# An output filled with the offset row before the normalised rows are added to it: the tail of a mixture-of-experts layer

## What is computed

```python
proj = x @ w_in                                  # 1024 x 2560
y    = concat(rg_lru(conv4(rg_x)) * gelu(rg_gate), sc_b * conv3(sc_c * sc_v))
h    = layer_norm(alpha * x + y @ w_out, ln1_g, ln1_b)
# router: the best of 4 groups, then the best 2 of its 8 experts; combine = their weights
hid  = silu(h @ exp_w_gate[e]) * (h @ exp_w_up[e]) * combine    # 32 experts, 1024 x 256 each
ffn  = sum_e hid_e @ exp_w_down[e]                              # 256 x 1024 each
out  = layer_norm(alpha * h + ffn, ln2_g, ln2_b)  # (z - mean) * rstd * ln2_g + ln2_b
```

## Time and profile before

| | |
|---|---|
| runs, median (lowest to highest) | 427.05 us (426.9 to 427.5) |
| the profiled execution, its own time | 426.65 us |
| its span in the trace | 424.9 us |
| granted TensorE clock over the span | 0.987 of 2.4 GHz |
| TensorE, VectorE, ScalarE, GpSimd busy | 96%, 48%, 22%, 21% of the span |
| moved by DMA | 137.03 MB, mean 323 GB/s |

### The profile page before, as it was taken

How to read it: one execution, slowest core, us unless ns; L and a number is a source line. 1 busy time by engine, 2 the same in 40 slices (tenths; PEclk the granted TensorE clock), 3 DMA queues, 4 the chain that set the end, 5 groups by cost and what they waited for, 6 DMA issues and landing times.

```text
span 424.9 us, 6858 instructions
## 1 busy us (share of the span) xinstructions
PE 406.7 (96%) x2734; PEld 277.6 (65%) x2734; DVE 205.6 (48%) x401; ACT 95.1 (22%) x148; POOL 89.4 (21%) x130
## 2 busy tenths in 40 slices
PE   6999999999999999998999999999999999798993
PEld 5888877888888888965556555555655655454541
DVE  1579622399957458775623322332332332232167
ACT  3533466984114001410000000000000000001031
POOL 3220000000000001053333233223323323311024
PEclk8999999999999999999999999999999999899998
DMA  8776421320269999989999999999999999999965
GB/s 275 243 216 199 150 89 61 99 79 21 99 202 398 420 422 414 422 343 410 417 416 416 412 415 413 412 416 415 413 417 419 416 415 419 416 420 413 395 267 197
DMA packets 37426, 137.03 MB, mean 323 GB/s; under 512 B 5155, under 2 KB 17475, under 8 KB 25366
## 3 DMA queue, kind: packets, MB, share of 16 engines
q1 hardware_dynamic: 31232, 124.79, 74.0%
q0 software_dynamic: 6144, 11.84, 7.8%
q10 hardware_dynamic: 22, 0.02, 0.0%
HBM read 132.31 MB, written 12.58 MB: 341 GB/s over the span
## 4 chain that ended last, share of the span: by engine, by line
PE 84%; DMA 10%; DVE 3%; SPq 1%; issue 1%; ACT 0%; POOL 0%; DVEq 0%; POOLq 0%
PE bank L1176 23%; PE bank L978 12%; PE bank L980 12%; PE bank L979 12%; PE bank L1205 11%; DMA wgu_spare<-in_exp_w_up 7%; PE bank L1164 3%; PE bank L1196 3%; PE bank L1221 2%; DMA xg<-h_rows,x_rows 2%; PE bank L1316 1%; PE bank L1075 1%; DMA raw<-in_w_in 1%; PE bank L1087 1%; PE bank L1038 1%
## 5 line engine op out<-in xcount | busy, mean ns | idle before, releaser
L1176 PE MATMUL bank<-wgu,xTg 128*64 128x256 f32 x736 | 86.0, 387 | 2.9 <-DMA wgu<-in_exp_w_up 2.9
L1176 PEld LDWEIGHTS bank<-wgu,xTg 128*64 128x64 f32 x736 | 51.6, 139 | 30.3 <-DMA wgu<-in_exp_w_up 3.2
L978 PE MATMUL bank<-xT_hi,w_hi 128*128 128x512 f32 x160 | 63.2, 395 | 1.7 <-DVE xT_lo L1380 1.7
L1699 DVE TENSOR_TENSOR hid<-hid,bank 64x256 f32<-64x256 f32 x32 | 13.5, 423 | 104.3 <-ACT hid L920 104.2
L980 PE MATMUL bank<-xT_hi,w_lo 128*128 128x512 f32 x160 | 62.8, 392 | 0.0
L979 PE MATMUL bank<-xT_lo,w_hi 128*128 128x512 f32 x160 | 62.8, 392 | 0.0
L743 POOL DMA_INDIRECT y_pairs<-xg,y_rows x32 | 31.9, 998 | 120.3 <-DVE xg L1709 114.5
L920 ACT ACTIVATE hid<-bank 64x256 f32<-64x256 f32 x32 | 12.0, 375 | 194.5 <-PE bank L1176 185.5
L1205 PE MATMUL bank<-wdn,hidT 128*64 128x512 f32 x192 | 45.4, 593 | 0.2 <-issue 0.2
L1357 DVE TENSOR_TENSOR w_lo<-raw,w_hi 128x2048 fp32r<-128x2048 f32 x12 | 27.5, 2289 | 26.9 <-ACT w_hi L834 26.7
L978 PEld LDWEIGHTS bank<-xT_hi,w_hi 128*128 128x128 f32 x160 | 30.2, 189 | 9.5 <-issue 3.4
(11 more groups left out here) (274 smaller groups left out, 497.3 us busy)
## 6 DMA issues: line engine op xcount, KB each, us to landing
wgu<-in_exp_w_gate SPq DMA_DIRECT2D x24, 1024.0 KB, 18.7
wgu<-in_exp_w_up SPq DMA_DIRECT2D x24, 1024.0 KB, 21.1
wdn<-in_exp_w_down SPq DMA_DIRECT2D x24, 1024.0 KB, 21.0
raw<-in_w_in SPq DMA_DIRECT2D x9, 1024.0 KB, 6.2
raw<-in_w_out SPq DMA_DIRECT2D x4, 1024.0 KB, 5.0
wdn_extra<-in_exp_w_down SPq DMA_DIRECT2D x4, 1024.0 KB, 20.7
wgu_spare<-in_exp_w_gate SPq DMA_DIRECT2D x4, 1024.0 KB, 21.7
wgu_spare<-in_exp_w_up SPq DMA_DIRECT2D x4, 1024.0 KB, 23.7
```

The source lines that it names most:

```text
L978: pe.matmul(dst, a_hi, b_hi, start=start, stop=False)
L1176: mm = pe.matmul(psum[2 + b][BLOCK * which:BLOCK * which + BLOCK, 0:F], xTg[b][:, j, h * BLOCK:(h + 1) * BLOCK], wgu[s][:, which, k, :], s ...
```

## The change

- SP issues eight stores inside the loop of chunk loads, behind chunks 4 to 11: each writes 64 rows of the output in HBM with the row `ln2_b`, 256 KB from HBM to HBM. The load of `ln2b` is gone.
- The normalised rows no longer get the offset on an engine. GpSimd issues the stores, with accumulation in the DMA (`accum_op=ALU.add`), onto the filled output. It waits once for the fills, and it ends with the wait for all stores.
- Columns 512 to 1023 of tiles 0 to 2, and columns 0 to 511 of tile 3, get their last scaling on ScalarE; the other half of tile 3 on VectorE. GpSimd has one operation for a tile where it had two.
- Item 31's gate and up pieces are loaded ahead of item 30's down weights. TensorE sums item 31's gate and up right behind item 30's, with item 30's transposition in the middle (`between`), and item 30's down behind that.
- The result of items 30 and 31 is kept as two fp32r parts, high by ScalarE and low by VectorE (`split_last`), and `last_hotT` is fp32r. Each of the two products of an `add_last` call becomes two, with one pass each. The four calls for item 30 and tiles 0 and 1, which stood around item 31's transposition, now come behind item 31's down.

```diff
             for c in range(1, N_CHUNKS):
...
+                if 4 <= c < 4 + 2 * TT:
+                    sp_.dma_start(out_rows[(c - 4) * BLOCK:(c - 3) * BLOCK, :], row(ln2_b).to_broadcast([BLOCK, D])).then_inc(out_filled, 16)
...
             refill_gu(N_EXP - 2)
-            refill_dn(N_EXP - 2)
             sp_.wait_ge(gu_summed, LAST - RING + 1)
...
+            refill_dn(N_EXP - 2)
             refill_dn(LAST)
...
-                    sp_.dma_start(ln2b[:, :], row(ln2_b).to_broadcast([P, D])).then_inc(ln2b_in, 16)
...
-            for t in range(TT - 1):
-                sp_.wait_ge(out_ready_pool, t + 1)
-                sp_.wait_ge(out_ready, t + 1)
-                sp_.dma_start(out_rows[t * P:(t + 1) * P, :], pair_y[2 * t + 1][:, :]).then_inc(out_stored, 16)
-            for h in range(2):
-                sp_.wait_ge(out_ready, TT + h)
-                cols = slice(h * H, (h + 1) * H)
-                sp_.dma_start(out_rows[(TT - 1) * P:, cols], pair_y[2 * TT - 1][:, cols]).then_inc(out_stored, 16)
-            sp_.wait_ge(out_stored, 16 * (TT + 1))
...
+            pool.wait_ge(out_filled, 16 * 2 * TT)
             for t in range(TT - 1):
...
-                pool.tensor_tensor(z, z, ln2b[:, 0:H], ALU.add).then_inc(out_ready_pool, 1)
+                pool.wait_ge(out_ready, t + 1)
+                pool.dma_start(out_rows[t * P:(t + 1) * P, :], z[:, :], accum_op=ALU.add).then_inc(out_stored, 16)
+            for h in range(2):
+                cols = slice(h * H, (h + 1) * H)
+                pool.wait_ge((out_ready, out_ready_last)[h], (TT, 1)[h])
+                pool.dma_start(out_rows[(TT - 1) * P:, cols], pair_y[2 * TT - 1][:, cols], accum_op=ALU.add).then_inc(out_stored, 16)
+            pool.wait_ge(out_stored, 16 * (TT + 1))
...
             rounds(act, act_item)
+            act.wait_ge(slot_weight_ready, 1)
+            copy_last(0)
             copy_last(1)
...
+                h = 0 if t == TT - 1 else 1
+                act.wait_ge(rstd2_ready, t + 1)
+                act.wait_ge(scaled2_ready, t + 1)
+                act.activation(pair_y[2 * t + 1][:, h * H:(h + 1) * H], z_of(t, h), ACT.Copy, scale=rstd[:, t:t + 1]).then_inc(out_ready, 1)
...
+                    if between is not None and k == KT // 2:
+                        between()
...
-                    pe.matmul(part_of(z_of(t, h), a), last_hotT[n][rows, t, :], last_y[n][rows, h * F:(h + 1) * F],
-                              start=first and turn == 0, stop=done is not None).then_inc(last_half_added if done is None else done, 1)
+                    pe.matmul(part_of(z_of(t, h), a), last_hotT[n][rows, t, :], last_y_hi[n][rows, h * F:(h + 1) * F],
+                              start=first and turn == 0, stop=False)
+                    pe.matmul(part_of(z_of(t, h), a), last_hotT[n][rows, t, :], last_y_lo[n][rows, h * F:(h + 1) * F],
+                              start=False, stop=done is not None).then_inc(last_half_added if done is None else done, 1)
...
                     gate_up(q, slot_of(q), q % 2, 2, loads_of(q, r))
-                    turn_hid(q, q % 2, 2)
                     return
                 if static(r) and q == LAST:
+                    gate_up(q, slot_of(q), q % 2, 2, loads_of(q, r), last_gu_in, lambda: turn_hid(q - 1, (q - 1) % 2, 2))
                     main_down(q - 1, r)
-                    gate_up(q, slot_of(q), q % 2, 2, loads_of(q, r), last_gu_in)
-                    pe.wait_ge(last_hotT_ready, 2)
-                    pe.wait_ge(last_y_copied, 1)
-                    add_last(0, 0, 0, True)
-                    add_last(0, 1, 0, True)
                     turn_hid(q, q % 2, 2)
-                    add_last(0, 0, 1, True)
-                    add_last(0, 1, 1, True)
                     return
...
             main_down(N_EXP - 1, 0)
+            pe.wait_ge(last_hotT_ready, 2)
+            pe.wait_ge(last_y_lo_ready, 1)
+            for turn in range(2):
+                for t in range(2):
+                    add_last(0, t, turn, True)
...
+            def split_last(n):
+                i = DIRECT[n]
+                v.wait_ge(last_y_hi_ready, n + 1)
+                v.scalar_tensor_tensor(out=last_y_lo[n][:, :], in0=psum[6 + i % 2][:, :], scalar=slot_weight[:, i:i + 1], in1=last_y_hi[n][:, :],
+                                       op0=ALU.mult, op1=ALU.subtract).then_inc(last_y_lo_ready, 1)
...
-                for h in halves:
-                    cols = slice(h * H, (h + 1) * H)
-                    v.scalar_tensor_tensor(out=pair_y[2 * t + 1][:, cols], in0=z_of(t, h), scalar=rstd[:, t:t + 1], in1=ln2b[:, cols],
-                                           op0=ALU.mult, op1=ALU.add).then_inc(out_ready, 1)
+                else:
+                    v.wait_ge(dve, chain[0])
+                    v.tensor_scalar(pair_y[2 * t + 1][:, H:D], z_of(t, 1), rstd[:, t:t + 1], None, ALU.mult).then_inc(out_ready_last, 1)
```

More of the change, by code:

```diff
@@ L255, in hybrid_moe_layer @@
         th = [tanhs[:, j, :] for j in range(3)] + [tanh3[:, :]]
-        last_hot = [at(f"last_hot{n}", [P, TT, 2, BLOCK], F32, ring + SLOT + 6144 * n) for n in range(2)]
-        last_hotT = [at(f"last_hotT{n}", [P, TT, P], F32, ring + SLOT + 6144 * n + 2048) for n in range(2)]
-        last_y = [at(f"last_y{n}", [P, H], F32, ring + SLOT + 6144 * n + 4096) for n in range(2)]
+        last_hot = [at(f"last_hot{n}", [P, TT, 2, BLOCK], F32, ring + SLOT + 8192 * n) for n in range(2)]
+        last_hotT = [at(f"last_hotT{n}", [P, TT, P], F32R, ring + SLOT + 8192 * n + 2048) for n in range(2)]
+        last_y_hi = [at(f"last_y_hi{n}", [P, H], F32R, ring + SLOT + 8192 * n + 4096) for n in range(2)]
+        last_y_lo = [at(f"last_y_lo{n}", [P, H], F32R, ring + SLOT + 8192 * n + 6144) for n in range(2)]
         ln2g = at("ln2g", [P, D], F32, ring + SLOT + 16384)
-        ln2b = at("ln2b", [P, D], F32, ring + SLOT + 20480)
         pair_y = [at(f"pair_y{u}", [P, D], F32, ring + 2 * SLOT + 4096 * u) for u in range(2 * TT)]
@@ L309, in hybrid_moe_layer @@
         ln2g_in = sem("ln2g_in")
-        ln2b_in = sem("ln2b_in")
+        out_filled = sem("out_filled")
         router_in = sem("router_in")
@@ L402, in hybrid_moe_layer @@
         last_hotT_ready = sem("last_hotT_ready")
-        last_y_copied = sem("last_y_copied")
+        last_y_hi_ready = sem("last_y_hi_ready")
+        last_y_lo_ready = sem("last_y_lo_ready")
         last_half_added = sem("last_half_added")
@@ L410, in hybrid_moe_layer @@
         out_ready = sem("out_ready")
-        out_ready_pool = sem("out_ready_pool")
+        out_ready_last = sem("out_ready_last")
+        scaled2_ready = sem("scaled2_ready")
+        rstd2_ready = sem("rstd2_ready")
         out_scaled = sem("out_scaled")
@@ L931, in act_item @@
                         act.activation(last_hotT[n][:, :, :], psum[n][:, :].rearrange("p (t n) -> p t n", t=TT), ACT.Copy).then_inc(last_hotT_ready, 1)
-                if static(r) and q == LAST:
-                    act.wait_ge(slot_weight_ready, 1)
-                    copy_last(0)
                 gate(q + r * RING, q % 2, 2)
             rounds(act, act_item)
+            act.wait_ge(slot_weight_ready, 1)
+            copy_last(0)
             copy_last(1)
@@ L1165, in turn_x, with gate_up @@
                 mm.then_inc(xg_turned, 1)
-            def gate_up(i, s, b, lag, loads, late=None):
+            def gate_up(i, s, b, lag, loads, late=None, between=None):
                 pe.wait_ge(gu_in[s], 32 * loads)
@@ L1744, in _ @@
             rounds(v, dve_item)
+            split_last(0)
+            split_last(1)
             def dve_over(j):
@@ L1769, in _ @@
                 for h in halves:
-                    step(v.scalar_tensor_tensor(out=z_of(t, h), in0=z_of(t, h), scalar=moments[:, t, 0:1],
-                                                in1=ln2g[:, h * H:(h + 1) * H], op0=ALU.subtract, op1=ALU.mult))
+                    ins = v.scalar_tensor_tensor(out=z_of(t, h), in0=z_of(t, h), scalar=moments[:, t, 0:1],
+                                                 in1=ln2g[:, h * H:(h + 1) * H], op0=ALU.subtract, op1=ALU.mult)
+                    if h == halves[0]:
+                        ins.then_inc(scaled2_ready, 1)
+                    else:
+                        step(ins)
                 v.wait_ge(dev2_ready, t + 1)
-                link(v.reciprocal(rstd[:, t:t + 1], rstd[:, t:t + 1]))
+                v.reciprocal(rstd[:, t:t + 1], rstd[:, t:t + 1]).then_inc(rstd2_ready, 1)
+                v.wait_ge(rstd2_ready, t + 1)
                 if t < TT - 1:
                     v.tensor_scalar(shift[:, t:t + 1], moments[:, t, 0:1], rstd[:, t:t + 1], -1.0, ALU.mult, ALU.mult).then_inc(moments2_ready, 1)
-                if t == 0:
-                    v.wait_ge(ln2b_in, 16)
-                for h in halves:
-                    cols = slice(h * H, (h + 1) * H)
```

(5 more changed lines are left out.)

11 lines of the change are left out of this document (5 added, 6 removed).

## The result

The changed kernel takes 430.25 us (median of 17 runs, 428.47 to 433.51) against 425.42 for the kernel before on the same chips (17 runs, 424.67 to 428.42). The ratio is 1.0096, with an interval of 1.0077 to 1.0114: slower by 4.1 us, and above the range. The profiled execution took 429.24, with a span of 427.5.

What follows compares the result with a forecast made beforehand. Bound: weight stream to 388.9, TensorE to 414.8, VectorE to 422.07, then the last store. Terms: -2.8 last statistics, -0.65 behind them, +0.54 second issue, +1.6 landing; gain 1.3, so 427.05 becomes 425.75 us; range 424.1 to 428.5.

Steps and rivals of the forecast that it cites:

- Fills: Eight output-filling stores on SP during the projections: predicted to cost nothing, with DMA engines 2 to 3 tenths busy.
- Reordering: Items 30 and 31 on TensorE: down of 31 ends at 402.2 instead of 404.27, a gain of 2.1 us.
- Additions: One-pass additions behind down of 31: 16 calls at 0.28, 4.5 us, plus 0.5 for waits.
- the first rival: TensorE's additions stay bound by weight loads: 16 calls take 7.6 us, not 5.0; time 428.2 us; chance 0.18.
- "0.2 (branch on the overflow count, less covered)": Term in TensorE's end sum of 415.0: the less covered branch behind the last items costs 0.2 us.
- "Behind it TensorE is the chain until 414.8": Kernel before, after item 30's weights land at 388.9: TensorE sets the time until 414.8, then VectorE until 422.07.
- GpSimd's second issue, at 419.2: Last tile's second store: its issue begins at 419.2, after the last value at 418.65 and a first issue of 0.54.
- The accumulating landing, 4.0: Last accumulating store: 4.0 us from issue to landing, taken between 2.6 and 6.7.
- The rival: Dear accumulation at the very last store: landing from 5.3 us on brings no gain, 6.7 gives 428.45 us; chance 0.12.
- "512 KB and 256 KB stores differ by 0.2 us, so bytes matter little when the stream is over": Argument against dear accumulation at the last store: store size barely changes the landing, by 0.2 us.
- 0.4 us to the end of the span: Term after the last store's landing: the span ends 0.4 us later.
- the forecast of 423.6: Predicted end of span: 419.2 + 4.0 + 0.4 = 423.6, a gain of 1.3 us against 424.9.

Runs made afterwards that it cites:

- no_fills: Changed kernel without the eight fills in the projections, stores still accumulating, so the output lacks its offset row; ratio 1.0103 to the kernel before, median 430.53 us.
- engines_add: Changed kernel's TensorE work with the old ending: offset added by VectorE and GpSimd, plain SP stores, no fills; ratio 1.0004 to the kernel before, 426.34 us.
- acc_last: Changed kernel with only the last tile's two stores accumulating; GpSimd stores tiles 0 to 2 plainly, without offset; ratio 1.0075 to the kernel before, 429.2 us.
- wait_on_sp: Changed kernel with the final wait for the stores on SP instead of GpSimd; ratio 1.0087 to the kernel before, median 430.06 us.
- pool_plain: Changed kernel with GpSimd's stores plain instead of accumulating, so the output lacks its offset; ratio 1.0038 to the kernel before, median 427.75 us.
- sp_plain: Changed kernel with plain stores issued by SP instead of accumulating ones by GpSimd, output without offset; ratio 0.9957 to the kernel before, median 424.17 us.
- gap_closed: sp_plain with item 30's four calls of additions moved behind the branch on the overflow count; ratio 0.9919 to the kernel before, median 422.02 us.
- engines_gap: engines_add with the four calls of additions moved behind the branch, computing the whole output; ratio 0.9971 to the kernel before, median 424.73 us.

## Why the prediction was wrong

Where it held:
- **Fills.** Nothing, as said (no_fills). The reading behind it was loose: in the slices from 32 to 105 us, where the fills are issued, has the DMA engines at 0 to 6 tenths, not at 2 to 3.
- **Reordering.** Down of 31 was to end 13.3 us behind item 30's start (402.2 less 388.9) and ended at 401.14 - 387.80 = 13.3. What was to be late next, item 30's down weights with a short wait, is there, 0.89 us at 396.40.
- **Additions.** 5.0 us for 64 records was the sum; the five stretches of them add up to 5.1 (1.27, 0.44, 1.51, 1.16 and 0.68), at 0.06 a record in the row and 0.1 to 0.2 more at each wait. This refutes the first rival, additions bound by weight loads. By the rule of the Trainium skill, "TensorE: Matmul & The Clock Gate", section "LDWEIGHTS (loading the stationary operand)", a load of 128 columns takes 107 ns, and the prediction had the rival right if that held for the spacing. Records that each load 128 columns, into alternating halves of the array's rows, follow at 60 ns here, so a load does not hold up the next record for its whole length, and the measurement decides. (That rival's own sum had a slip of 0.2: 423.6 and 2.6 more are 426.2, not 426.0.)

Where it failed, in order of place:
- **"0.2 (branch on the overflow count, less covered)".** It measured 1.69. The prediction named the cover, but not what it is made of: the moved additions replaced 1.9 us of queued work that depends on nothing by short records with waits among them. Those 1.5 us are more than the head's loss of 0.8, so they are what turned its gain into a loss. TensorE's end was to come 26.1 us behind item 30's start and came at 415.57 - 387.80 = 27.8.
- **"Behind it TensorE is the chain until 414.8".** The old ending's pace was VectorE's as much, 3.27 us a tile; the prediction took the engine in the chain for the only pace. The sum took no harm, since the new ending frees VectorE too, but this is why the tensor part alone (engines_add) gives nothing in the tail.
- **GpSimd's second issue, at 419.2.** It began at 419.9. The last values came at 418.9 to 419.0 and not at 418.65 (0.3), GpSimd issued 0.37 behind them (the chain's last issue row), and its second issue began 0.6 behind the first. An accumulating issue, 0.90 and 1.24, is also longer than the 0.54 of the earlier trace rows.
- **The accumulating landing, 4.0.** It measured 6.2 for the last one. For one store with no accumulation ahead, 4.0 is what acc_last measured; since it was chosen between two rows of other kinds of transfer, the hit is partly luck. What the term left out is what stands ahead. With the last tile alone accumulating, the second store already needs 5.6, since it waits for the first; the whole tiles ahead add the other 0.6. The rival had this mechanism and this size, 6.7 at the dear end, with a chance of 0.12. What failed is the sentence that held the chance down: "512 KB and 256 KB stores differ by 0.2 us, so bytes matter little when the stream is over". Those 0.2 us were read from plain stores. Accumulating ones run at 200 and 128 GB/s, and the 2.1 MB of output keep the engines full for over 10 us. The term should have been a rate, asked of all bytes in flight, not a distance asked of one store.
- **0.4 us to the end of the span.** It measured 1.4, with the last store and the wait on GpSimd. What the extra microsecond consists of stays open beyond the half that wait_on_sp shows.

The tail's sum against the forecast of 423.6: 0.7 for the later second issue, 2.2 for the landing, 1.0 for the end, together 3.9, which is 427.5. The gap's 1.5 does not appear among them, because item 30 started 1.1 us early in this profile. By the ratio the two kernels differ by 4.1 us, the two profiled spans by 2.6; the early start makes up 1.1 of that distance.

In parts, from the ratios: accumulating costs 2.5 us (after less pool_plain), GpSimd in SP's place 3.4 (pool_plain less sp_plain; some of it may be clock after the gap), and the open branch 1.6 (sp_plain less gap_closed). Together that is 7.5. By their intervals each of these parts is uncertain by 1.1 to 1.5 us; the profiles give 3.3, 2.1 (without the clock) and 1.6. Without these three the change would gain 3.5 us (gap_closed, which leaves the offset out), with them it loses 4.1. Giving the offset back to VectorE and GpSimd costs 2.2 of the 3.5 (engines_gap less gap_closed).

## What to carry to other kernels

An accumulating store is not a free addition: take its rate from a run (here half that of a plain store, and less for the half-width stores of the last tile), divide all the bytes of the last stage by it, and compare with the pace of the engine that it relieves; here 0.7 us of VectorE a tile was exchanged for DMA engines that stayed full past the end. Before moving work across a branch that reads a register, look at what is queued in front of the branch without waits in it; put short records with waits behind it. And before costing the last tiles, read the spacing of one operation over all of them, not the engine that stands in the chain once.

## What the runs showed of the hardware

- Accumulating DMAs into HBM ran at about 200 GB/s for whole tiles (rows of 4 KB) and 128 GB/s for half-width ones (rows of 2 KB), with all 16 engines full, against some 400 GB/s for plain stores. They landed in 5.1 to 6.4 us, or 4.0 for one of 256 KB with no accumulation ahead, and held up plain stores of another queue (4.7 instead of 2.2).
- GpSimd's issue took 0.86 to 1.24 us with the addition and 0.54 to 0.64 without.
- The span ended 1.4 to 1.65 us behind the last landing when GpSimd issued the last store and waited for it, 0.9 when SP waited, and 0.4 when SP did both.
- Reading the count and branching on TensorE's sequencer left the array idle for 1.37 to 1.70 us with short records in front, and not at all behind 1.94 us of long ones. The Trainium skill, "Runtime: NRT & Kernel Launch", section "Instruction fetch mechanics", says that a taken branch out of the fetched window must wait for its code; that could be it, and no run here shows it.
- One of nine profiles with that gap shows TensorE's granted clock at its lower level for about 3 us behind it, at a cost of 1.56 us. All fourteen show such a stretch once between 368 and 382 us, behind a wait of 2.1 to 2.7 us for weights, in which 32 products of gate and up took 5.1 to 5.4 us instead of 3.67; in six of them the first of two such waits passed without it.
